# A compressed bias built through DRAM, position weights as the moving operand, and one source for a norm's mean

## The chip, the cores and the metric

The kernel runs on one core of one Trainium2 chip. The metric is the time of one execution on the device, in microseconds (us). Lower is better.

## What is computed

The program is a two-layer decoder step for 512 prompt tokens and 64 new tokens (8 sequences of 8), 576 tokens together, with a stream of 1024 features. Layer 0 is a Mamba-2 mixer with an MLP, layer 1 a sparse attention mixer with an MLP. After each of the four halves stands a post-layer-norm. What the change touches, cut to its core:

```
def layer_norm(x, g, b):
    mu = jnp.mean(xf, axis=-1, keepdims=True)
    var = jnp.mean(jnp.square(xf - mu), axis=-1, keepdims=True)
    return ((xf - mu) * lax.rsqrt(var + LN_EPS)).astype(x.dtype) * g + b

# compression of 32 tokens into one: (token + position vector pe) times w1, per k and v
hid = einsum('bcjgd,jde->bcge', chunks[:, 0:n_cmp] + pe[0:CMP_STRIDE][:, None, :], w1[0]) + (the same for r = 1)
return einsum('bcge,ed->bcgd', silu(hid), w2)

# compressed branch of the attention: a bias by distance, from a table of 32 buckets x 16 heads
s_c = einsum('qgrd,cgd->qgrc', qq, kc) * scale
s_c = s_c + bias_hgr[rel_bucket(pos[:, None] - cmp_end[None, :])]
```

The position vectors' share of the hidden layer, pe times w1, is one vector of 128 for k and one for v: it is summed once and then added as a bias ("position sums").

## The kernel before

**Weights.** All dense products run in `dense_block` (L1247 to L1274). Weights come from DRAM in 512 KB slots. The SP queue loads a slot into one of two `ring` buffers (`stream`, L594 to L599), ScalarE (ACT) rounds it into `split[:, j, 0]` (`split_hi`, L932), GpSimd (POOL) writes the remainder into `split[:, j, 1]` (`split_lo`, L673), and TensorE (PE) then runs 48 matmuls on the slot. So at most four slots are on the way: two in `split`, two in `ring`. SP issues a load only when POOL has split what the ring buffer held, and it issues in program order: any other DMA in its list stands between two slots.

**Bias tables.** Between the first quarter of MLP 0 (its first hidden half) and the second, `bias_tables` (L1503 to L1519) makes on PE first a table `bt` of heads x distances (3 matmuls, L1510) and then the compressed bias `cbt`: 56 matmuls, each with a shifted window of 128 distances of the one-hot table `ef` as the stationary operand and the 32 x 16 bucket table `relb` as the moving one (L1517). VectorE (DVE) copies both out (L2013 to L2019). The next dense block follows on PE at once. SP meanwhile stores `bt` to the DRAM scratch `bscr` (L611), copies it into a skewed table `bskew` (L615), loads strips `Rs` of that (L619) and then 16 small pieces `nr`, one for each head (L624), with slots of weights between these steps. `cbt` is read in the attention, after 1390 us.

**Norms.** `last_projection` (PE), `finish_his` (ACT), `finish_los` (POOL) and `last_residuals` (DVE) build the stream's last eight chunks of 128 features (`xT[:, m]`) with their squares. DVE adds chunks 0 to 6 into `row` while they come. `layer_norm` on PE sums by token (12 short passes for six matmuls, each with 96 tokens as the stationary operand: L1290) `row` and chunk 7 into two columns of `s1`, and the squares into `s2`; spreads the mean over all partitions (L1496, L1497: `row` and chunk 7 accumulate in `flat_x`), and spreads the scale (L1501) when DVE and ACT have computed the variance (L1970 to L1977). DVE then works through eight chunks (L1982, L1985), ACT writes them in two forms (L1106, L1107), and POOL the remainder (L794). Norm k = 1 stands between MLP 0 and the shared K/V projection.

**Position sums.** Their weights `cw1` (2 MB) lie where the bias tables' `ef`, `eb` and `bt` did, and POOL issues the load (L840) behind all its splits of the slots up to norm 1. `position_sums` on PE then stands between the pieces of the first K/V block: 32 matmuls with a 128 x 128 piece of `cw1` as the stationary operand and a single column of `cpe` as the moving one (L1545); PE waits for `cw1` ahead of that block. ACT copies the result as `hpe` (L1110), and PE waits for it before the second block.

An fp32 matmul is two passes of a weight load and a matmul in the trace, so "x112" there is 56 matmuls of the program.

Of the kernel before, what the change touches and what calls it, by code (L numbers as in the profile page):

```python
# [27 lines left out]
ALU = mybir.AluOpType  # L28
ACT = mybir.ActivationFunctionType
AX = mybir.AxisListType  # L30

P = 128
# [53 lines left out]
def build(nc, a):  # L86

    with ExitStack() as ctx:
# [131 lines left out]
        at[0] = KC * T  # L220
        bd = carve(512)
# [54 lines left out]
        CEN, SQS = zip(*((v[:, 0, :], v[:, 1, :]) for v in (spare, spare_x, spare, spare_x)))  # L276
        ptab = sb("ptab", [1, NB * NPG], I32)
# [215 lines left out]
        s1 = dense[0:TQ, 0, 0:2 * TC].rearrange("p (c k) -> p c k", k=2)  # L493
# [96 lines left out]
        def _(sp):  # L590
# [3 lines left out]
            def stream(first, last):  # L594
                with sp.Fori(first // NSLOT, last // NSLOT) as i:
                    for j in range(NSLOT):
# [23 lines left out]
                         ).then_inc(strips_loaded, 16)  # L620
            stream(s_bias + 2 * NSLOT, s_bias + 3 * NSLOT)
            sp.wait_ge(strips_loaded, 16)
# [20 lines left out]
        def _(pool):  # L643
# [194 lines left out]
            pool.wait_ge(cbt_ready, 1)  # L838
# [78 lines left out]
        def _(act):  # L917
# [180 lines left out]
            def layer_norm(k):  # L1098
# [9 lines left out]
                if k == 1:  # L1108
                    act.wait_ge(pe_done, 1)
                    act.activation(hpe, dense[:, 3, 0:2], ACT.Copy).then_inc(hpe_ready, 1)  # L1110
# [133 lines left out]
        def _(pe):  # L1244
# [31 lines left out]
            def projection(b0, s0, blocks, nsl, hi, lo, ready=None, rounded=None, after=None):  # L1276

                for j in range(2):
                    dense_block(b0 + j, s0 + j * nsl, nsl, hi, lo, ready=ready if j == 0 else None,
                                rounded=rounded if j == 0 else None, after=after if j == 0 else None)  # L1280
                    if after and j == 0:
                        pe.wait_ge(hpe_ready, 1)
# [202 lines left out]

            def layer_norm(k):

                b0 = ENDS[k][0]
                pe.wait_ge(ln_sum, 6 * (k + 1))
                by_token(s1, 0, row)  # L1490
                pe.wait_ge(blk_evac, b0 + KC)
                by_token(s1, 1, xT[:, KC - 1, :]).then_inc(ln_tok, 1)
                pe.wait_ge(ln_sq, (k + 1) * KC)
                by_token(s2, 1, sq[:, 1, :]).then_inc(ln_tok, 1)
                for cols in (slice(0, 512), slice(512, T)):
                    pe.matmul(flat_x[:, cols], onesd[:, :], row[:, cols], start=True, stop=False)  # L1496
                    mm = pe.matmul(flat_x[:, cols], onesd[:, :], xT[:, KC - 1, cols], start=False, stop=True)  # L1497
                mm.then_inc(ln_wide, 1)
                pe.wait_ge(ln_stats, 2 * k + 2)
                for cols in (slice(0, 512), slice(512, T)):  # L1500
                    mm = pe.matmul(flat_s[:, cols], ones[0:TQ, :], SQS[k][0:TQ, cols], start=True, stop=True)  # L1501
                mm.then_inc(ln_wide, 1)

            def bias_tables():
# [9 lines left out]
                for i in range(NSIG):  # L1514
                    o_ = i * NH
                    x0 = X0 + CB0 - CS * i
                    mm = pe.matmul(bS[:, o_ // 512, o_ % 512:o_ % 512 + NH], ef[:, x0:x0 + P], relb[:, :],  # L1517
                                   start=True, stop=True)
# [19 lines left out]
            pe.wait_ge(s_cw1, 16)  # L1538

            def position_sums(k):  # L1540


                for j in range(5 * k, min(5 * k + 5, 32)):
                    kv, i = divmod(j, 16)
                    mm = pe.matmul(dense[:, 3, kv:kv + 1], cw1[:, kv, i // 8, i % 8, :],  # L1545
                                   cpe[:, kv, i // 8, i % 8:i % 8 + 1], start=i == 0, stop=i == 15)
                if k == KC - 2:
                    mm.then_inc(pe_done, 1)

            projection(B_KV, S_KV, SL_KV, 1, x_h, x_l, (x_split, 2 * KC), (xh_ready, KC), position_sums)
# [43 lines left out]
            def compressed(s_):  # L1596
                pe.wait_ge(hpe_ready, 1)
# [178 lines left out]
        def _(dve):  # L1776
# [168 lines left out]
            def last_residuals(k):  # L1945
# [13 lines left out]
                for m in range(2, KC):  # L1959
# [3 lines left out]
                    if m < KC - 1:  # L1963
                        dve.wait_ge(blk_evac, b0 + m + 1)
                        dve.wait_ge(ln_sum, 6 * k + m - 1)
# [447 lines left out]
```

## Time and profile before

| | us |
|---|---|
| median of 3 runs | 2146.24 (2142.49 to 2151.03) |
| the profiled execution's own time | 2147.33 |
| its span, first to last instruction | 2145.7 |
| PE busy in it | 1982.5 (92%) |
| PE weight loads | 1817.4 (85%) |
| DVE busy | 866.9 (40%) |
| ACT busy | 652.0 (30%) |
| POOL busy | 973.5 (45%) |
| mean granted TensorE clock | 0.937 of full |

The share of PE tells that the kernel is PE's nearly everywhere; what a change is worth is read from the stretch in which it stands. A granted clock of 1.00 is TensorE's 2.4 GHz, 0.50 is 1.2 GHz.

### The profile page before, as it was taken

Reading aid. Unit: us, or ns where it says so; the run is one execution under the profiler, and the core shown is the slowest. Engines: PE = TensorE matmul, PEld = TensorE weight load, DVE = VectorE, ACT = ScalarE, POOL = GpSimd, SP = SyncE. Lnnn points to the kernel's source line nnn. Section 1 sums busy time; section 2 is a strip of 40 time slices with the busy share of each in tenths; the row PEclk is TensorE's granted clock in tenths of the full one; section 3 lists DMA queues with packets and bytes.
Section 4 is the critical chain, followed back from the end, with each engine's and each line's share of the span. In section 5 each row is a group of like instructions: output and inputs, shape, how many; then the busy total and the mean of one; then the engine's idle time right before and its main releaser. Section 6 shows DMA issues by size and latency. Waiting matters only on the chain.

```text
span 2145.7 us, 36763 instructions
## 1 busy us (share of the span) xinstructions
PE 1982.5 (92%) x14824; PEld 1817.4 (85%) x14824; DVE 866.9 (40%) x1712; ACT 652.0 (30%) x1115; POOL 973.5 (45%) x697
## 2 busy tenths in 40 slices
PE   7989898978979998999999998989978999999997
PEld 5988887857778998999998998955547899999996
DVE  7484766847455210012233112167745621002134
ACT  3443343432133211122223113166634422112222
POOL 2444445446437642356453333344412565345552
PEclk9999999978998988999996998989999899999998
DMA  4211213122131215322221243350060122222221
GB/s 167 71 50 64 104 40 119 50 81 92 50 114 60 81 67 127 100 79 80 87 79 69 79 152 116 87 204 1 21 236 25 56 79 86 81 79 88 79 79 64
DMA packets 52629, 184.61 MB, mean 86 GB/s; under 512 B 7070, under 2 KB 11838, under 8 KB 50976
## 3 DMA queue, kind: packets, MB, share of 16 engines
q1 hardware_dynamic: 40272, 129.66, 18.3%
q0 software_dynamic: 9952, 50.08, 6.5%
q10 hardware_dynamic: 2288, 3.23, 0.4%
q8 instruction: 84, 1.38, 0.3%
q14 instruction: 33, 0.27, 0.0%
HBM read 166.59 MB, written 27.28 MB: 90 GB/s over the span
## 4 chain that ended last, share of the span: by engine, by line
PE 68%; DVE 12%; issue 9%; POOL 5%; ACT 4%; DMA 1%; ACTq 0%; SPq 0%; POOLq 0%; DVEq 0%
PE dense L1269 48%; PE dense L1592 3%; POOL split L673 3%; DVE tile L1908 2%; PE dense L1675 2%; PE bS L1381 2%; DVE tile L1818 2%; PE dense L1632 1%; PE bXM L1662 1%; POOL tile L780 1%; POOL hid L805 1%; PE bXM L1443 1%; PE bXM L1388 1%; PE dense L1710 1%; DVE tile L1811 1%
## 5 line engine op out<-in xcount | busy, mean ns | idle before, releaser
L1269 PE MATMUL dense<-xs,split 128*128 128x288 f32 x6848 | 984.7, 302 | 32.3 <-DVE y_lo L1936 9.2
L1269 PEld LDWEIGHTS dense<-xs,split 128*128 128x128 f32 x6848 | 948.7, 193 | 64.5 <-issue 51.7
L673 POOL TENSOR_TENSOR split<-ring,split 128x1024 fp32r<-128x1024 f32 x212 | 533.6, 2517 | 846.6 <-ACT split L932 825.4
L932 ACT ACTIVATE split<-ring 128x1024 fp32r<-128x1024 f32 x212 | 224.6, 1059 | 830.5 <-PE dense L1269 816.1
L1269 PE MATMUL dense<-hid,split 128*128 128x288 f32 x3072 | 417.1, 298 | 6.0 <-POOL split L673 6.0
L1269 PEld LDWEIGHTS dense<-hid,split 128*128 128x128 f32 x3072 | 415.6, 191 | 6.3 <-POOL split L673 6.3
L1830 DVE SCALAR_TENSOR_TENSOR tile<-tile,dense 128x576 f32<-128x576 f32 (+1 forms) x56 | 42.2, 754 | 422.9 <-PE dense L1269 422.9
L1995 DVE TENSOR_SCALAR sq<-dense 128x576 f32<-128x576 f32 x64 | 48.5, 758 | 310.5 <-PE dense L1269 310.5
L903 POOL TENSOR_SCALAR tile<-tile,tile,tile 128x128 f32<-128x128 f32 (+3 forms) x128 | 78.3, 626 | 80.1 <-DVE tile L2159 80.1
L805 POOL TENSOR_TENSOR hid<-sq,hid 128x576 f32 x64 | 77.2, 1206 | 0.0
L1171 ACT ACTIVATE tile<-tile,tile 128x128 f32<-128x128 f32 (+3 forms) x128 | 70.5, 553 | 18.2 <-DVE tile L2144 18.0
L1818 DVE SCALAR_TENSOR_TENSOR tile<-tile,tile,tile 128x512 f32<-128x512 f32 x72 | 69.5, 966 | 2.6
L1592 PE MATMUL dense<-tile,tile 128*128 128x128 f32 x576 | 66.4, 274 | 0.8 <-issue 0.8
L1592 PEld LDWEIGHTS dense<-tile,tile 128*128 128x128 f32 x576 | 64.9, 188 | 1.9 <-issue 1.2
L1960 DVE SCALAR_TENSOR_TENSOR tile<-tile,tile 128x576 f32<-128x576 f32 x24 | 61.8, 2575 | 0.0
L1118 ACT ACTIVATE hid<-sq 128x576 f32 x64 | 44.0, 687 | 44.3 <-DVE sq L1998 44.3
L1269 PE MATMUL dense<-y_lo,split 128*128 128x288 f32 x256 | 56.1, 301 | 0.0
L1908 DVE SCALAR_TENSOR_TENSOR tile<-tile,tile,tile 128x128 f32<-128x128 f32 (+1 forms) x80 | 53.8, 734 | 0.7
L1632 PE MATMUL dense<-tile,tile 64*128 64x128 f32 (+3 forms) x128 | 47.8, 491 | 6.2 <-DVE tile L2136 4.6
L1675 PE MATMUL dense<-tile,tile 128*64 128x256 f32 x384 | 51.8, 391 | 0.0
L1998 DVE TENSOR_TENSOR sq<-sq 128x576 f32<-128x576 f32 x64 | 48.5, 758 | 2.2
L1632 PE MATMUL bS<-tile,tile 64*128 64x128 f32 (+3 forms) x128 | 48.9, 495 | 0.4 <-DVE tile L2099 0.4
(316 smaller groups left out, 2174.0 us busy)
## 6 DMA issues: line engine op xcount, KB each, us to landing
ring<-in_w SPq DMA_DIRECT2D x212, 512.0 KB, 3.3
tile<-in_state POOLq DMA_DIRECT2D x4, 2048.0 KB, 9.4
o_sssm<-tile POOLq DMA_DIRECT2D x4, 2048.0 KB, 7.5
tile<-in_cmp POOLq DMA_DIRECT2D x32, 256.0 KB, 3.3
tile<-in_win POOLq DMA_DIRECT2D x8, 1024.0 KB, 6.0
tile<-in_sel SPq DMA_DIRECT2D x32, 256.0 KB, 5.1
o_kv<-tile POOLq DMA_DIRECT2D x1, 3456.0 KB, 14.1
bskew<-bscr SPq DMA_DIRECT2D x1, 3072.0 KB, 22.6
```

Source lines behind the costliest of these rows:

```text
L673: pool.tensor_tensor(split[:, j, 1, :], ring[:, j, :], split[:, j, 0, :].bitcast(F32), ALU.subtract).then_inc(w_split, 1)
L805: pool.tensor_tensor(hid[:, 1, m, :], sq[:, j, :], hid[:, 0, m, :].bitcast(F32), ALU.subtract).then_inc(hid_ready, 1)
L903: last = pool.tensor_scalar(pb(u, r)[:, 0:n], pb(u, r)[:, 0:n], wt[:, u % 2, r:r + 1], gate, ALU.mult, ALU.mult)
L932: act.activation(split[:, j, 0, :], ring[:, j, :], ACT.Copy).then_inc(w_hi, 1)
L1171: last = act.activation(pb(u, r)[:, 0:n], pb(u, r)[:, 0:n], ACT.Exp, bias=nmx[:, u % 4, r:r + 1], accum_out=sm[:, u % 4, r:r + 1])
L1269: mm = pe.matmul(dense[:, 2 * par + h_, 0:HT], split[:, j, w, cols], v[:, kk, h_ * HT:(h_ + 1) * HT], start=kk == 0 and t == 0, stop=kk == ...
L1592: mm = pe.matmul(dense[:, 2 * (s_ % 2) + kv, r * P:(r + 1) * P], cw1[:, kv, r, j, :], rows, start=j == 0, stop=j == 7)
L1632: pe.matmul(SB[k][:, 0:(qt + 1) * P], qT[half_of(h_), gp * GR + r, tok(qt)], kvT[half_of(h_), 4 * (br + 1) + gp, 0:(qt + 1) * P], start=Tr ...
L1675: mm = pe.matmul(OBANK[half_of(g), rr * 2 * P:(rr + 1) * 2 * P], v, PT[t % 4][:, h_ * 2 * P:(h_ + 1) * 2 * P], start=br == 0 and kt == 0, ...
L1818: dve.scalar_tensor_tensor(o[:, 0:NP_TOK], r[:, k:k + NP_TOK], cw[:, x, k:k + 1], o[:, 0:NP_TOK], ALU.mult, ALU.add)
L1908: last = dve.scalar_tensor_tensor(yt[:, j * L:(j + 1) * L], xg[:, j, tok(c)], dsk[:, g * 4 + j:g * 4 + j + 1], yt[:, j * L:(j + 1) * L], A ...
L1960: link(dve, "dve", dve.scalar_tensor_tensor(xT[:, m, :], xT[:, m, :], alpha, CEN[k], ALU.mult, ALU.subtract))
```

## The change

Three parts.

1. **Compressed bias.** PE makes 8 matmuls with windows of `ef` that don't overlap, so that a table `btT` of distances x heads results (1024 x 16). DVE copies it out once. SP stores it to `bscr` (rows of 64 bytes) when the skewed table has been made from the old contents, right behind the load of `Rs`, and two slots later waits for that store and issues 56 loads, each of 128 rows of 64 bytes, into `cbt`. DVE waits for them in the attention. POOL's wait ahead of `cw1` now names the matmuls' end.
2. **Position sums.** The column of `cpe` is stationary and 128 columns of `cw1` move. The 32 matmuls stand in norm 1 on PE: 3 behind the last residual, 13 behind the spread mean, 16 behind the spread scale. PE's wait for `cw1` stands ahead of the first 3. The result is one row; ACT copies it to `posr`, and behind the first K/V block two matmuls turn it into two columns, which ACT copies to `hpe`; PE waits for both.
3. **Mean.** DVE adds chunk 7 to `row` as well; PE sums by token and spreads the mean from `row` alone, behind the sums of squares.

```diff
             sp.dma_start(Rs, bass.AP(a["bskew"].tensor, P - 1, [[NH * RW - 1, P], [RW, NH], [1, RB]])
                          ).then_inc(strips_loaded, 16)
+            sp.wait_ge(bt_ready, 2)
+            sp.dma_start(bass.AP(a["bscr"].tensor, 0, [[NH, P], [NH * P, 8], [1, NH]]), btT).then_inc(bt_stored, 16)
             stream(s_bias + 2 * NSLOT, s_bias + 3 * NSLOT)
+            sp.wait_ge(bt_stored, 32)
+            for i in range(NSIG):
+                sp.dma_start(cbt[:, i, :], bass.AP(a["bscr"].tensor, (X0 + CB0 - CS * i) * NH, [[NH, P], [1, NH]])
+                             ).then_inc(cbt_ready, 16)
             sp.wait_ge(strips_loaded, 16)
...
-            pool.wait_ge(cbt_ready, 1)
+            pool.wait_ge(cbt_done, 1)
...
                     act.wait_ge(pe_done, 1)
+                    act.activation(posr[0:1, :], dense[0:1, 2, 0:2 * P], ACT.Copy).then_inc(hpe_ready, 1)
+                    act.wait_ge(pe_done, 2)
                     act.activation(hpe, dense[:, 3, 0:2], ACT.Copy).then_inc(hpe_ready, 1)
...
+                    if b0 == B_KV and j == 0:
+                        position_columns()
+                        pe.wait_ge(hpe_ready, 2)
...
+            def position_sums(first, last):
+                for j in range(first, last):
+                    kv, i = divmod(j, 16)
+                    mm = pe.matmul(dense[0:1, 2, kv * P:(kv + 1) * P], cpe[:, kv, i // 8, i % 8:i % 8 + 1],
+                                   cw1[:, kv, i // 8, i % 8, :], start=i == 0, stop=i == 15)
+                if last == 32:
+                    mm.then_inc(pe_done, 1)
+            def position_columns():
+                pe.wait_ge(hpe_ready, 1)
+                for kv in range(2):
+                    mm = pe.matmul(dense[:, 3, kv:kv + 1], posr[0:1, kv * P:(kv + 1) * P], ones[0:1, 0:1],
+                                   start=True, stop=True)
+                mm.then_inc(pe_done, 1)
+            def fill(k, place):
+                if k == 1:
+                    if place == 0:
+                        pe.wait_ge(s_cw1, 16)
+                    position_sums(*((0, 3), (3, 16), (16, 32))[place])
             def layer_norm(k):
                 b0 = ENDS[k][0]
-                pe.wait_ge(ln_sum, 6 * (k + 1))
-                by_token(s1, 0, row)
                 pe.wait_ge(blk_evac, b0 + KC)
-                by_token(s1, 1, xT[:, KC - 1, :]).then_inc(ln_tok, 1)
+                fill(k, 0)
                 pe.wait_ge(ln_sq, (k + 1) * KC)
                 by_token(s2, 1, sq[:, 1, :]).then_inc(ln_tok, 1)
+                pe.wait_ge(ln_sum, 7 * (k + 1))
+                by_token(s1, 0, row).then_inc(ln_tok, 1)
                 for cols in (slice(0, 512), slice(512, T)):
-                    pe.matmul(flat_x[:, cols], onesd[:, :], row[:, cols], start=True, stop=False)
-                    mm = pe.matmul(flat_x[:, cols], onesd[:, :], xT[:, KC - 1, cols], start=False, stop=True)
+                    mm = pe.matmul(flat_x[:, cols], onesd[:, :], row[:, cols], start=True, stop=True)
                 mm.then_inc(ln_wide, 1)
+                fill(k, 1)
...
                 mm.then_inc(ln_wide, 1)
+                fill(k, 2)
...
-                for i in range(NSIG):
-                    o_ = i * NH
-                    x0 = X0 + CB0 - CS * i
-                    mm = pe.matmul(bS[:, o_ // 512, o_ % 512:o_ % 512 + NH], ef[:, x0:x0 + P], relb[:, :],
+                for i in range(8):
+                    mm = pe.matmul(bS[:, 0, i * NH:(i + 1) * NH], ef[:, i * P:(i + 1) * P], relb[:, :],
                                    start=True, stop=True)
...
-                    if m < KC - 1:
-                        dve.wait_ge(blk_evac, b0 + m + 1)
-                        dve.wait_ge(ln_sum, 6 * k + m - 1)
-                        dve.tensor_tensor(row[:, :], row[:, :], xT[:, m, :], ALU.add).then_inc(ln_sum, 1)
+                    dve.wait_ge(blk_evac, b0 + m + 1)
+                    dve.wait_ge(ln_sum, 7 * k + m - 1)
+                    dve.tensor_tensor(row[:, :], row[:, :], xT[:, m, :], ALU.add).then_inc(ln_sum, 1)
             def layer_norm(k):
                 dve.wait_ge(ln_tok, 3 * k + 2)
-                link(dve, "dve", dve.tensor_reduce(lnt[:, 0, :], s1, AX.X, ALU.add))
-                link(dve, "dve", dve.tensor_tensor(lnt[:, 1, :], lnt[:, 0, :], lnt[:, 0, :], ALU.mult))
+                dve.tensor_reduce(lnt[:, 0, :], s2, AX.X, ALU.add)
                 dve.wait_ge(ln_tok, 3 * k + 3)
-                link(dve, "dve", dve.tensor_reduce(lnt[:, 0, :], s2, AX.X, ALU.add))
+                link(dve, "dve", dve.tensor_copy(lnt[:, 1, :], s1[:, :, 0]))
+                link(dve, "dve", dve.tensor_tensor(lnt[:, 1, :], lnt[:, 1, :], lnt[:, 1, :], ALU.mult))
```

SP's list around the bias tables, before (ring loads are slots of weights, `tile_137` is `Rs`, `tile_117` is `nr`):

```order
L615 DMA bskew<-bscr 2048x1x384
L595 UNCONDITIONAL_BRANCH
L599 DMA ring<-in_w 128x1024 x2
L595 REGISTER_ALU
L595 COMPARE_AND_BRANCH
L619 DMA tile_137<-bskew 128x16x256
L595 UNCONDITIONAL_BRANCH
L599 DMA ring<-in_w 128x1024 x2
L595 REGISTER_ALU
L595 COMPARE_AND_BRANCH
L624 DMA tile_117<-tile_137 8x144 x16
```

The same place of SP's list after the change (`tile_138` is now `Rs`, `tile_118` is `nr`, `tile_115` is `btT`, `tile_132` is `cbt`):

```order
L623 DMA tile_138<-bskew 128x16x256
L626 DMA bscr<-tile_115 128x8x16
L599 UNCONDITIONAL_BRANCH
L603 DMA ring<-in_w 128x1024 x2
L599 REGISTER_ALU
L599 COMPARE_AND_BRANCH
L630 DMA tile_132<-bscr 128x16 x56
L634 DMA tile_118<-tile_138 8x144 x16
L599 UNCONDITIONAL_BRANCH
```

One DMA more stands between two pairs of slots, and 56 more ahead of the 16 that stood there.

PE's list at norm 1, before (`tile_154` holds the summed squares and then the scale, `tile_49` is the stream, `tile_118` is `cpe` and `tile_126` is `cw1`):

```order
L1290 MATMUL dense<-onesd,row 96x1 x6
L1290 MATMUL dense<-onesd,tile_49 96x1 x6
L1290 MATMUL dense<-onesd,sq 96x1 x6
L1496 MATMUL bXM<-row,onesd 128x512
L1497 MATMUL bXM<-tile_49,onesd 128x512
L1496 MATMUL bXM<-row,onesd 128x64
L1497 MATMUL bXM<-tile_49,onesd 128x64
L1501 MATMUL bS<-tile_154,ones 128x512
L1501 MATMUL bS<-tile_154,ones 128x64
L1269 MATMUL dense<-xs,split 128x288 x6
L1545 MATMUL dense<-tile_126,tile_118 128x1 x5
L1269 MATMUL dense<-xs,split 128x288 x6
```

And after the change (`tile_119` is now `cpe`, `tile_127` is `cw1`, `tile_155` the scale):

```order
L1281 MATMUL dense<-hid,split 128x288 x6
L1504 MATMUL dense<-tile_119,tile_127 1x128 x3
L1303 MATMUL dense<-onesd,sq 96x1 x6
L1303 MATMUL dense<-onesd,row 96x1 x6
L1533 MATMUL bXM<-row,onesd 128x512
L1533 MATMUL bXM<-row,onesd 128x64
L1504 MATMUL dense<-tile_119,tile_127 1x128 x13
L1538 MATMUL bS<-tile_155,ones 128x512
L1538 MATMUL bS<-tile_155,ones 128x64
L1504 MATMUL dense<-tile_119,tile_127 1x128 x16
L1281 MATMUL dense<-xs,split 128x288 x48
L1513 MATMUL dense<-ones,row 128x1 x2
```

The position sums moved from inside the first K/V block into the norm, the sums by token of `row` behind those of the squares, and those of the stream's last chunk are gone.

## Rows read from the trace of the kernel before

**Rows 1.** The page: busy us, share of the span and instructions of each engine.

```profile
PE 1982.5 (92%) x14824; PEld 1817.4 (85%) x14824; DVE 866.9 (40%) x1712; ACT 652.0 (30%) x1115; POOL 973.5 (45%) x697
```

**Rows 2.** Timeline 780:818, bias tables: start us, us, engine line op [idle <-releaser].

```profile
787.01 23.10 PE L1517 MATMUL bS<-tile,tile 128*128 128x16 f32 x112 [1.45 <-DVE tile L2015]
...
809.95 8.30 PE L1269 MATMUL dense<-hid,split 128*128 128x288 f32 x42
```

**Rows 3.** Windows: stretch, its length, PE, PEld, DVE, ACT, POOL busy, PEclk, DMA share, GB/s.

```profile
788.00:789.50 1.50, 1.50 (x10) 1.50 (x9) 0.00 (x0) 0.00 (x0) 0.65 (x1) 0.54 0.55 126
...
809.90:815.00 5.10, 5.10 (x23) 5.10 (x23) 1.16 (x2) 0.00 (x0) 0.00 (x0) 0.50 0.00 0
```

**Rows 4.** SP's own timeline, 780:960 (same columns).

```profile
852.21 0.39 SPq L619 DMA_DIRECT2D tile<-bskew  x1
857.04 2.65 SPq L599 DMA_DIRECT2D ring<-in_w  x2
860.93 10.86 SPq L624 DMA_DIRECT2D tile<-tile  x16
872.15 82.05 SPq L599 DMA_DIRECT2D ring<-in_w  x14
```

**Rows 5.** Timeline of all engines, 826:905.

```profile
857.07 48.16 PE L1269 MATMUL dense<-hid,split 128*128 128x288 f32 x338 [6.02 <-POOL split L673]
...
873.11 0.76 DVE L1830 SCALAR_TENSOR_TENSOR tile<-tile,dense 128x576 f32 x1 [21.14 <-PE dense L1269]
...
885.80 1.06 ACT L932 ACTIVATE split<-ring 128x1024 fp32r<-128x1024 f32 x1 [5.34 <-PE dense L1269]
...
886.94 2.38 POOL L673 TENSOR_TENSOR split<-ring,split 128x1024 fp32r<-128x1024 f32 x1 [4.02 <-ACT split L932]
```

**Rows 6.** DMA issues: out<-in, engine, KB each, us to landing.

```profile
ring<-in_w SPq DMA_DIRECT2D x212, 512.0 KB, 3.3
...
tile<-bskew SPq DMA_DIRECT2D x1, 2048.0 KB, 8.7
...
tile<-in_nw ACTq DMA_DIRECT2D x1, 8.0 KB, 6.6
tile<-in_dsk ACTq DMA_DIRECT2D x1, 8.0 KB, 6.3
```

**Rows 7.** Timeline of ACT, 0:40: its DMA issues at the start.

```profile
7.71 0.47 ACTq L923 DMA_DIRECT2D tile<-in_nw  x1
8.21 0.65 ACTq L923 DMA_DIRECT2D tile<-in_dsk  x1
```

**Rows 8.** The chain that ended last, 1120:1180, in order of time.

```profile
1136.11 9.52 DMA tile<-in_cw
```

**Rows 9.** Timeline of norm 1 and the first K/V block, 1119:1200.

```profile
1133.48 2.06 PE L1290 MATMUL dense<-onesd,sq 128*96 128x1 f32 x12
...
1139.70 1.25 PE L1501 MATMUL bS<-tile,ones 96*128 96x512 f32 x4
...
1178.88 1.06 ACT L932 ACTIVATE split<-ring 128x1024 fp32r<-128x1024 f32 x1 [6.57 <-PE dense L1269]
```

**Rows 10.** Windows around norm 1 (columns as in Rows 3).

```profile
1145.60:1171.20 25.60, 25.52 (x113) 25.53 (x114) 6.25 (x9) 8.66 (x13) 8.82 (x8) 0.50 0.00 1
```

**Rows 11.** Timeline of norm 0, 648:700.

```profile
670.65 1.95 PE L1501 MATMUL bS<-tile,ones 96*128 96x512 f32 x4
...
687.66 1.06 ACT L932 ACTIVATE split<-ring 128x1024 fp32r<-128x1024 f32 x1 [1.91 <-PE dense L1269]
```

**Rows 12.** Timeline of the last norm, 2117:2146.

```profile
2121.73 1.23 PE L1290 MATMUL dense<-onesd,tile 128*96 128x1 f32 x12
...
2126.59 1.91 PE L1497 MATMUL bXM<-tile,onesd 128*128 128x512 f32 x2
...
2128.30 0.53 PE L1496 MATMUL bXM<-row,onesd 128*128 128x64 f32 x2
...
2129.05 1.50 PE L1501 MATMUL bS<-tile,ones 96*128 96x512 f32 x4
```

More of the change, by code:

```diff
@@ L220, in build @@
         at[0] = KC * T
+        btT = carve(8, NH)
+        at[0] = KC * T
         bd = carve(512)
@@ L276, in build @@
         CEN, SQS = zip(*((v[:, 0, :], v[:, 1, :]) for v in (spare, spare_x, spare, spare_x)))
+        posr = row[0:1, 0:2 * P]
         ptab = sb("ptab", [1, NB * NPG], I32)
@@ L492, in build @@
         flat_s = bS.rearrange("p a b -> p (a b)")[:, 0:T]
-        s1 = dense[0:TQ, 0, 0:2 * TC].rearrange("p (c k) -> p c k", k=2)
+        s1 = dense[0:TQ, 0, 0:TC].unsqueeze(2)
         s2 = dense[0:TQ, 1, 0:2 * TC].rearrange("p (c k) -> p c k", k=2)
@@ L1274, in dense_block, with projection @@
                     mm.then_inc(w_used, 1)
-            def projection(b0, s0, blocks, nsl, hi, lo, ready=None, rounded=None, after=None):
+            def projection(b0, s0, blocks, nsl, hi, lo, ready=None, rounded=None):
                 for j in range(2):
                     dense_block(b0 + j, s0 + j * nsl, nsl, hi, lo, ready=ready if j == 0 else None,
-                                rounded=rounded if j == 0 else None, after=after if j == 0 else None)
-                    if after and j == 0:
-                        pe.wait_ge(hpe_ready, 1)
+                                rounded=rounded if j == 0 else None)
+                    if b0 == B_KV and j == 0:
+                        position_columns()
+                        pe.wait_ge(hpe_ready, 2)
                 with pe.Fori(1, blocks // 2) as i:
@@ L1536, in _ @@
             layer_norm(1)
[L1538 to L1552, printed above, removed]
+            projection(B_KV, S_KV, SL_KV, 1, x_h, x_l, (x_split, 2 * KC), (xh_ready, KC))
             projection(B_Q, S_Q, SL_Q, 1, x_h, x_l)
@@ L1596, in compressed @@
             def compressed(s_):
-                pe.wait_ge(hpe_ready, 1)
+                pe.wait_ge(hpe_ready, 2)
                 if s_:
@@ L2016, in _ @@
             dve.wait_ge(cbt_done, 1)
-            flat = cbt.rearrange("p s h -> p (s h)")
-            dve.tensor_copy(flat[:, 0:512], bS[:, 0, :])
-            dve.tensor_copy(flat[:, 512:NSIG * NH], bS[:, 1, 0:NSIG * NH - 512]).then_inc(cbt_ready, 1)
+            dve.tensor_copy(btT.rearrange("p s h -> p (s h)"), bS[:, 0, 0:8 * NH]).then_inc(bt_ready, 1)
             residuals(B_M2[0][0], S_M2[0][0], 2, ALPHA)
@@ L2094, in shift_compressed @@
                 dve.wait_ge(pcs_done, qt + 1)
+                dve.wait_ge(cbt_ready, 16 * NSIG)
                 s0 = 24 - 8 * qt
```

## The prediction

> **What bounds the kernel now.** I read the page first: PE is busy 92% of the span [rows 1], so an edit is worth what it takes from PE's line, or what it makes PE wait. Then the timeline of each of three places. At the bias tables PE spends 23.1 us on the 56 shifted matmuls, and the next dense block starts when they end, at 809.95 [rows 2]: all of this is on the path. SP's own timeline behind it shows a queue that already costs something: the load of `Rs` is issued at 852.21, two slots at 857.04, then 16 small DMAs that hold SP for 10.86 us, and the next slot goes out at 872.15 [rows 4]. PE waits 6.02 us for a split slot at 857.07, behind the transfer of the skewed table, but not for the 16 small DMAs [rows 5]: four slots are on the way and cover them. At norm 1 the chain of waits runs through a DMA, not through the norm: `cw1` goes out at 1136.11 and takes 9.52 us, to 1145.63 [rows 8], while the norm's scale was spread by 1140.95 [rows 9]. From there to the end of the first K/V block PE is full for 25.60 us at granted clock 0.50, that is 1.2 GHz [rows 10]; where nothing stands between its pieces, the same block ends 15.1 us behind the spread scale (norm 0: 672.6 to 687.66) [rows 11].
>
> **Part 1a, the matmuls.** 56 become 8, or 112 passes 16. Over all of them a pass takes 23.1 / 112 = 0.206 us [rows 2], early on, partly at full clock, 1.5 / 10 = 0.15 [rows 3]. I take 16 x 0.15 = 2.4, so PE comes free at 789.4: **-20.5 us** (-19.8 by the other pace). Behind the tables the dense block runs at clock 0.50 for 5.1 us [rows 3], which costs some 2.6 us. The clock fell in the first two microseconds of these narrow matmuls, and the 8 lie in them, so I leave that loss as it is; the bound is another -2.6.
>
> **Part 1b, the loads on SP.** I work in the times of the trace of before; the shift is common to all that follows. The store of `btT` goes out behind `Rs` at about 852.7 and can't land before it, 852.21 + 8.7 = 860.9 [rows 4, 6]. Its 1024 rows at the pace of the 2048 rows of `Rs` would add 4.3; the rows are short, I take 863.5 (860.9 to 866). Two slots go out in between as before, at 857.04 and 859.4. Then SP waits for the store and issues 56 loads. What one costs SP no row shows for this queue; the nearest are two loads of the same shape, 128 rows of 64 bytes, that ACT issues in a row at the start: 0.47 and 0.65 us, starts 0.50 apart [rows 7]. `Rs` holds SP 0.39, the 16 pieces 10.86 / 16 = 0.68 each [rows 4]. I take 0.48, nearest to the same shape and a little off it because SP's single issues are shorter: 56 x 0.48 = 26.9 us, to 890.4. The 16 pieces follow, 10.9 us, to 901.3. Only then does the next slot go out: 3.3 us to landing [rows 6], ACT 1.06 and POOL 2.38 [rows 5], with gaps 908.2. PE has worked through its four slots at 885.8 (ACT's rounding starts when the block ends) [rows 5]. So PE waits **22.4 us**. Behind the wait of 6.02 the block of two slots lasts 857.07 to 873.1, 16.0 us, against 12.7 for the one behind it [rows 5]: the clock falls in the wait and costs 3.2. Sum +25.6; with 0.42 for an issue +22.2, with 0.68 +36.8, and the store's landing adds -2.6 to +2.5. The loads themselves land long before `cbt` is read, and DVE's new wait costs nothing.
>
> A rule of the Trainium skill speaks to this (DMA: Bandwidth & Descriptors, Issuing engines are not separate DMA queues): the time that it takes to initiate a DMA on the sequencer is usually small beside the DMA. Here it is the other way: the two small loads land at 7.71 + 6.6 = 14.3 and 8.21 + 6.3 = 14.5, 0.2 us apart, while their issue takes 0.5 [rows 6, 7]. By the rule the 56 would cost what they take to move, 11 us, not 27, and the stall would be 16 us shorter; that is the third rival below.
>
> **Part 1 together:** -20.5 + 25.6 = **+5.1 us**.
>
> **Part 2, norm 1.** What is moved: 64 passes out of the K/V block, into the norm. What moves with them is PE's wait for `cw1`. It stood ahead of the block, it now stands ahead of the sums of squares, and everything in the norm is queued behind it. POOL still issues the load at 1136.1, behind its last split. PE's chain, in the times of before: `cw1` at 1145.6; a 512-column pass at half clock is 1.71 / 2 = 0.85 [rows 12], so one of 128 columns is 0.21 and half of that at full clock; the weight load of one column hides beside it. Three sums, 6 passes: 1.3, to 1146.9. Squares by token 2.06 and `row` by token 2.06 [rows 9], to 1151.0. The mean spread from `row` alone: 1.71 + 0.37 = 2.1 [rows 12], to 1153.1. Then 13 sums, 26 passes: 5.5 at half clock, 2.8 at full; PE has been busy with wide passes for some time by then, I take 4.2, to 1157.3. The scale, which DVE has ready before that, is spread by 1158.5 (1.25 [rows 9]). Before it was 1140.95: **17.6 us later**. The last 16 sums lie beside DVE's first chunks. The block ends 15.1 behind, as at norm 0, at 1173.6; the two column matmuls and ACT's copy, which PE waits for, are some 0.9, so the second block starts at 1174.5 and ends 6.4 later, at 1180.9 (half of the 12.7 of two slots). Before, that end was 1178.88 [rows 9]. So the block's relief of some 14 us is spent on the wait: **+2.0 us**, between +0.6 (full clock) and +4.
>
> **Part 3, the other three norms.** The chunk-7 sums by token took 1.23 and two wide passes 1.71 plus two narrow 0.37 [rows 12]; `row`'s sums by token, formerly hidden beside DVE's last residual, come onto the line with 2.06. In the last norm the scale's spread began 7.3 us behind the last residual, at 2129.05. Now: the square 0.7, squares by token 2.0, `row` 2.0, spread mean 2.1, in sum 6.8; and behind `row`'s sums DVE and ACT need about as long for the scale, 2.1. So -0.3 each, **-1.0 us**. DVE's added row sum lies beside ACT's square and PE's sums of squares. If the scale's chain is met by other work on DVE, +1 each; if PE gets its clock back earlier, -1 each.
>
> **The sum:** +5.1 + 2.0 - 1.0 = +6.1 us on the profiled execution's 2147.33, that is 2153.4. The median of the runs shown is 1.1 lower, so I predict **2152.3**. A change of under 0.5%, 10.7 us, is about what a measurement of this kernel can't tell from none. The forecast's own range, from 0.42 to 0.55 us an issue and the clock, is 2144 to 2159.
>
> **Rivals.** (A) A dear issue: SP takes for each of the 56 what it takes for each of the 16 pieces, 0.68. Then the wait is 56 x 0.20 = 11.2 longer: 2163.5. For it: the same queue, many in a row, short rows. Against: those pieces have SBUF on both sides and only 8 partitions. From 0.57 an issue on the result is beyond 0.5%. Chance 0.28; with a late store it reaches 2168. (B) The four slots cover more than I think and the norm's wait vanishes, because `cw1` lands before the norm: then its sums fill waits, the block ends near 1159 instead of 1173.6, and the time is 2138. Against it is POOL's order, where nothing has moved ahead. Chance 0.05. (C) A cheap issue, at the pace of landing, 0.20: 56 x 0.28 = 15.7 less, 2136.6. For it only that the transfers are that quick; against it every row of an issue here, none under 0.39 [rows 4, 7]. Chance 0.1, a part of it with a gain of over 0.5%. (D) That the change doesn't save the 20 us of PE: nothing speaks for that, since the matmuls are gone from the list; what could eat it is another wait in the same stretch, of a size no row gives. 0.02.
>
> **How the numbers follow.** Forecast 0.55, A 0.28, C 0.1, B 0.05, D 0.02. Within 0.5% lie the forecast, B and most of C; above it A, save its low end, and a tail of the forecast. Faster 0.1, same 0.62, slower 0.28. The range takes in C's edge and A with its late store: 2137 to 2168.
>
> **What would show it.** In the profile after: the dense block behind the tables starts some 20.5 us earlier; SP's timeline shows the 56 in 27 us; PE waits some 22 us for a split, and over 3 at half clock follow; in norm 1 PE waits for `cw1` behind the last residual, for 13 us, and the scale is spread 17 to 18 us later against that residual. The prediction is wrong if an issue costs clearly less or more than 0.48, or if the store of 1024 short rows takes much longer than `Rs`.

## The result, and the profile after

| | before | changed |
|---|---|---|
| median of 19 runs each, us | 2147.22 (2141.58 to 2156.2) | 2154.33 (2146.24 to 2159.42) |
| span of the profiled execution, us | 2145.7 | 2144.6 |
| PE busy in it, us | 1982.5 | 1938.6 |
| mean granted TensorE clock | 0.937 | 0.942 |

The ratio is 1.0031, 95% interval 1.0019 to 1.0043: the changed kernel is slower by 0.3%, or 2147.22 x 0.0031 = 6.7 us (the two medians lie 7.1 apart). The sum had given +6.1. That is less than the 0.5% that the prediction took as the limit of what can be told from none, but 19 runs of each do show the sign.

The page's first rows would tell another story. This is the row of the changed kernel that answers to [rows 1]:

```profile
PE 1938.6 (90%) x14668; PEld 1775.3 (83%) x14668; DVE 864.2 (40%) x1715; ACT 652.8 (30%) x1116; POOL 972.8 (45%) x697
```

PE is busy 44 us less, and nothing is gained. The busy time that went has come back as idle time of the same engine, and two new waits, of 22.6 and 14.6 us, are the most of it (an old wait of 4.7 us for `cw1` went). The view of PE's waits, 775 to 1180, changed kernel (total us, times, longest):

```profile
PE dense L1281 <- POOL split L683: 29.3, 2, 22.6
PE dense L1504 <- DMA tile<-in_cw: 14.6, 1, 14.6
```

The two profiled executions can't be compared as wholes either: the changed one is 1.1 us shorter in its span. It is ahead by 5.5 us before the first changed step of weight. DVE's timeline shows the last residual ahead of norm 0 in the kernel before and then in the changed one:

```profile
662.96 0.75 DVE L1830 SCALAR_TENSOR_TENSOR tile<-tile,dense 128x576 f32<-128x576 f32 x1 [3.53 <-PE dense L1269]
```

```profile
657.43 0.75 DVE L1852 SCALAR_TENSOR_TENSOR tile<-tile,dense 128x576 f32<-128x576 f32 x1 [3.53 <-PE dense L1281]
```

The code up to there (the Mamba half) is the same on PE, so those 5.5 us are nothing that the change did. So I compare stretches between landmarks that both programs have, and take the total from the ratio of many runs. All kernels of this study, by those stretches of their profiled executions (us; "norm 1" is from its last residual to DVE's first copy of the second K/V block; "scale" is from that residual to DVE's first multiplication by the scale):

| kernel | ratio to before, 95% | tables to norm 1 | norm 1 | scale |
|---|---|---|---|---|
| before | 1 | 344.3 | 47.7 | 9.72 |
| changed | 1.0031 [1.0019, 1.0043] | 349.8 | 49.75 | 27.15 |
| p1_alone | 1.0027 [1.0008, 1.0045] | 345.4 | 46.8 | 8.16 |
| p23_alone | 0.9996 [0.9974, 1.0018] | 342.3 | 49.9 | 27.32 |
| late | 0.9910 [0.9881, 0.9939] | 321.6 | 50.2 | 27.63 |
| one_load | 0.9886 [0.9851, 0.9921] | 322.6 | 50.3 | 27.69 |
| cw1_early | 0.9946 [0.9926, 0.9967] | 344.3 | 31.7 | 9.17 |
| best_late | 0.9826 [0.9800, 0.9852] | 321.5 | 36.6 | 14.01 |
| before_cw1_early | 0.9980 [0.9958, 1.0002] | 340.7 | 45.0 | 9.71 |
| p1_late_cw1 | 0.9872 [0.9848, 0.9896] | 323.8 | 45.2 | 9.72 |
| best_one | 0.9842 [0.9812, 0.9872] | 322.4 | 33.4 | 10.83 |
| best_places | 0.9835 [0.9802, 0.9869] | 321.8 | 33.0 | 9.04 |

Each row of stretches is one execution, and not always a middling one. The changed kernel's profiled execution, 2146.24 us, is the quickest of its 19; cw1_early's took 2130.6 (median of its runs 2139.16), and p1_late_cw1's 2131.58 is the slowest of its six (median 2121.95). Behind the bias tables the same 8 matmuls were followed by 6 us at a granted clock of 0.50 in the changed kernel, 0.55 in p1_late_cw1, 0.72 to 0.78 in six other kernels and 1.00 in p1_alone, so between 0 and 3 us of any first stretch is that clock alone.

**The bias tables and SP.** All engines' timeline, 775 to 935, changed kernel, the rows that answer to [rows 2] and [rows 5] (start us, us, engine, line, operation, in brackets idle time and what ended it):

```profile
781.19 2.37 PE L1553 MATMUL bS<-tile,tile 128*128 128x16 f32 x16 [1.45 <-DVE tile L2036]
...
783.39 41.41 PE L1281 MATMUL dense<-hid,split 128*128 128x288 f32 x288
...
831.50 28.48 PE L1281 MATMUL dense<-hid,split 128*128 128x288 f32 x192 [6.70 <-POOL split L683]
...
882.55 41.27 PE L1281 MATMUL dense<-hid,split 128*128 128x288 f32 x288 [22.57 <-POOL split L683]
...
898.38 0.76 DVE L1852 SCALAR_TENSOR_TENSOR tile<-tile,dense 128x576 f32 x1 [37.48 <-PE dense L1281]
```

The 8 matmuls take 2.2 us from their start to the next block's (781.19 to 783.39), where the 56 took 22.94. The wait of 6.02 is still there, as 6.70. Behind it stands the new one, 22.57 us, and it is ended by a split slot. SP's own timeline, 770 to 990, says why (same columns, answers to [rows 4]), and the view of SP's waits, 820 to 900, adds what it waited for ahead of the 56:

```profile
826.68 0.39 SPq L623 DMA_DIRECT2D tile<-bskew  x1
827.12 2.42 SPq L626 DMA_DIRECT2D bscr<-tile  x1
...
837.26 26.71 SPq L630 DMA_DIRECT2D tile<-bscr  x56
864.01 10.85 SPq L634 DMA_DIRECT2D tile<-tile  x16
875.24 110.63 SPq L603 DMA_DIRECT2D ring<-in_w  x19
```

```profile
SPq L630 <- DMA bscr<-tile: 2.9, 1, 2.9
```

From the load of `Rs` to the next slot behind the 16 pieces it was 19.9 us (852.21 to 872.15), and it is 48.6 (826.68 to 875.24). The 28.6 us more are 26.7 for the 56 issues, 26.71 / 56 = 0.477 us each, and the rest is the wait for the store, 2.9 us where SP had waited 1.2 us ahead of the 16 pieces before (857.04 + 2.65 = 859.69, and they go out at 860.93).

**Norm 1.** All engines' timeline 1112 to 1182, changed kernel (answers to [rows 9] and [rows 8]):

```profile
1130.99 0.76 DVE L1852 SCALAR_TENSOR_TENSOR tile<-tile,dense 128x576 f32<-128x576 f32 x1 [9.44 <-PE dense L1281]
...
1135.77 0.56 POOL L850 DMA_DIRECT2D tile<-in_cw  x1
1145.50 1.44 PE L1504 MATMUL dense<-tile,tile 128*1 128x128 f32 x6 [14.62 <-DMA tile<-in_cw]
1146.87 2.08 PE L1303 MATMUL dense<-onesd,sq 128*96 128x1 f32 x12
1148.81 2.06 PE L1303 MATMUL dense<-onesd,row 128*96 128x1 f32 x12
...
1150.73 2.38 PE L1533 MATMUL bXM<-row,onesd 128*128 128x512 f32 x4
...
1153.04 3.77 PE L1504 MATMUL dense<-tile,tile 128*1 128x128 f32 x26
...
1156.74 1.29 PE L1538 MATMUL bS<-tile,ones 96*128 96x512 f32 x4
...
1158.14 0.76 DVE L2006 TENSOR_TENSOR tile<-tile,bS 128x576 f32<-128x576 f32 x1 [4.24 <-PE bS L1538]
...
1173.26 0.76 DVE L2048 TENSOR_SCALAR tile<-dense 128x576 f32 x1 [4.18 <-PE dense L1281]
...
1173.88 8.28 PE L1281 MATMUL dense<-xs,split 128*128 128x288 f32 x60 [0.26 <-ACT tile L1122]
```

PE stands 14.62 us for `cw1` with the whole norm behind that wait. The scale comes 27.15 us behind the last residual instead of 9.72. The first K/V block, without the position sums in it, makes up all but 2.05 us of that: its result is copied 15.12 us behind the scale (1158.14 to 1173.26), where it was 30.33 before.

That 15.1 is the same in all eight kernels with part 2 (15.07 to 15.12 us), with 16 or with 24 sums standing ahead of the block on PE. PE doesn't set it: in the changed kernel it waits seven times, mostly 0.45 us, for the next chunk's remainder from POOL (3.0 us in sum in the view of waits). ACT sets it: it writes each chunk in its two forms, 0.76 us apart and without a gap (ACT's timeline 1160 to 1168), so one chunk comes every 1.52 us. With the sums inside, PE was the bound of the block, busy for 25.52 of 25.60 us [rows 10].

**The last norm.** PE's timeline 2110 to 2146, changed kernel (answers to [rows 12]):

```profile
2122.46 1.15 PE L1303 MATMUL dense<-onesd,sq 128*96 128x1 f32 x12 [1.72 <-ACT sq L960]
2123.47 1.59 PE L1303 MATMUL dense<-onesd,row 128*96 128x1 f32 x12
2124.93 2.37 PE L1533 MATMUL bXM<-row,onesd 128*128 128x512 f32 x4
2127.09 2.35 PE L1538 MATMUL bS<-tile,ones 96*128 96x512 f32 x4
```

The sums by token of chunk 7 and its two wide passes (512 and 64 columns) are gone. From the last residual to the scale it is 8.71 us, before it was 9.73; at norm 0 9.43 against 9.75, at norm 2 10.07 against 9.74. Part 3 was never run alone, and 0.3 us a norm is far below what the runs can tell, so its worth is read from profiles only.

### The profile page after: what moved, and what is told of

Read it like the earlier page. It is cut to its first block and busy times, and to the rows that moved or that the text cites. A ratio compares the mean times of both kernels' runs of the same rounds, so it can differ in the third digit from the quotient of the medians.

```text
span 2144.6 us, 36515 instructions
## 1 busy us (share of the span) xinstructions
PE 1938.6 (90%) x14668; PEld 1775.3 (83%) x14668; DVE 864.2 (40%) x1715; ACT 652.8 (30%) x1116; POOL 972.8 (45%) x697
```

## The experiments

My theory: part 1 gives 21 us on PE and loses a little more than that to SP's 56 issues; part 2's gain is spent on the wait for `cw1`, since POOL issues that load behind its last split. Rivals: the 56 cost by what they move, not by their issue; SP's queue is slowed by something else (the store); the moved sums save nothing of their own.

**Each half alone.** p1_alone is the kernel before with part 1; p23_alone is the changed kernel without it. What parts them, cut short (+ as in p1_alone and the changed kernel):

```diff
+            sp.dma_start(bass.AP(a["bscr"].tensor, 0, [[NH, P], [NH * P, 8], [1, NH]]), btT).then_inc(bt_stored, 16)
...
+            for i in range(NSIG):
+                sp.dma_start(cbt[:, i, :], ...)
...
-                for i in range(NSIG):
-                    mm = pe.matmul(bS[:, o_ // 512, o_ % 512:o_ % 512 + NH], ef[:, x0:x0 + P], relb[:, :], ...)
+                for i in range(8):
+                    mm = pe.matmul(bS[:, 0, i * NH:(i + 1) * NH], ef[:, i * P:(i + 1) * P], relb[:, :], ...)
```

> The kernel before with part 1 alone (8 matmuls, table of distances through DRAM, 56 loads on SP). Theory (SP's issue of the 56 loads starves TensorE of slots): the 56 take 26.7 us on SP, PE waits 22 to 23 us for a split and then runs some 3 us longer at half clock; the matmuls give back 20.7; between the start of the bias tables and the last residual of norm 1 the trace grows by 5.5 us, from 344.3; ratio to before 1.0025. Rival (the loss of the whole change comes from norm 1): no growth here, ratio 0.991 to 1.000.

> The change without part 1 (position sums in norm 1 and the mean from one source alone). Theory: between the bias tables and the last residual of norm 1 the 344.3 us of before; from that residual to the end of the second K/V block 49.6 us against 47.6 before; the three other norms -1.0 in sum; ratio 1.0005. Rival (the wait for cw1 costs more than the block gets back): 1.003 or more.

Measured: p1_alone 1.0027 [1.0008, 1.0045], p23_alone 0.9996 [0.9974, 1.0018]. Both ratios came as expected. As far as the runs can tell, the loss is part 1's: its interval lies above 1, that of parts 2 and 3 around 1. In p1_alone SP holds the 56 for 26.70 us and PE waits 22.0 us at the one place; p23_alone has only the old wait. The view of PE's waits, 785 to 1150, of p1_alone and then of p23_alone:

```profile
PE dense L1277 <- POOL split L681: 28.3, 2, 22.0
```

```profile
PE dense L1495 <- DMA tile<-in_cw: 14.6, 1, 14.6
PE dense L1272 <- POOL split L674: 5.6, 1, 5.6
```

From tables to norm 1 the profile of p1_alone is 1.1 us longer than before, not 5.5 as the changed kernel's. The clock accounts for some 3 of that: behind the 8 matmuls it stayed at 1.00 in p1_alone and fell to 0.50 in the changed kernel, on the same instructions; the two waits for slots are 1.0 us shorter in sum. The windows of that stretch, p1_alone and then changed (stretch, length, busy us of PE, PEld, DVE, ACT, POOL, then the granted clock, DMA share, GB/s):

```profile
788.00:794.00 6.00, 6.00 (x48) 6.00 (x47) 0.10 (x1) 0.00 (x0) 0.00 (x0) 1.00 0.23 86
```

```profile
783.40:789.30 5.90, 5.90 (x25) 5.90 (x26) 0.29 (x1) 0.00 (x0) 0.00 (x0) 0.50 0.20 74
```

**The issue or the transfer?** Two kernels keep all that part 1 computes and moves. late puts the 56 loads behind all weights of the stretch, where `cbt` is still not needed for long; one_load leaves them where they are, but as one DMA of the same 7168 rows of 64 bytes.

```diff
 # late
-            sp.wait_ge(bt_stored, 32)
-            for i in range(NSIG):
-                sp.dma_start(cbt[:, i, :], ...)
             sp.wait_ge(strips_loaded, 16)
...
             stream(s_bias + 3 * NSLOT, S_O + 2 * NSLOT)
+            sp.wait_ge(bt_stored, 32)
+            for i in range(NSIG):
+                sp.dma_start(cbt[:, i, :], ...)
 # one_load
-            for i in range(NSIG):
-                sp.dma_start(cbt[:, i, :], bass.AP(a["bscr"].tensor, (X0 + CB0 - CS * i) * NH, [[NH, P], [1, NH]])
-                             ).then_inc(cbt_ready, 16)
+            sp.dma_start(cbt, bass.AP(a["bscr"].tensor, (X0 + CB0) * NH, [[NH, P], [-CS * NH, NSIG], [1, NH]])
+                         ).then_inc(cbt_ready, 16)
```

> The changed kernel; SP issues the 56 loads behind its last slot ahead of the attention, where it is idle, not between slots. Theory (SP's queue): PE's wait of 22.6 us and the half clock behind it go, the stretch from the bias tables to the last residual of norm 1 falls from 349.8 to 324 us; ratio to before 0.991. Rival (the store of btT or the DMA engines' load of short rows hold the slots): over 335 us.

> The changed kernel with one DMA of 7168 rows in place of the 56 of 128, same bytes, same place. Theory (what holds the slots is SP's time per issue): the wait of PE shrinks by what SP saves against 26.7 us. The store of btT, 1024 rows in one DMA, held SP 2.42 us; by that pace the one load holds it 17 us and PE waits some 13 us; by the 0.39 us of the load of Rs it waits 0 to 3 us. Rival (the DMA engines' time for 7168 short rows holds the slots): PE waits 20 us or more, whatever SP's issue takes, and the slot behind lands late.

Measured: late 0.9910 [0.9881, 0.9939], one_load 0.9886 [0.9851, 0.9921]. The intervals overlap, so the two can't be told apart. The new wait is gone in both, and from tables to norm 1 they take 321.6 and 322.6 us against 349.8. PE's waits up to norm 1, late and then one_load:

```profile
PE dense L1281 <- POOL split L683: 5.9, 1, 5.9
```

```profile
PE dense L1280 <- POOL split L682: 6.4, 1, 6.4
```

And SP's timeline of one_load, with the landing of the one load from the view of DMA issues (KB, us to landing):

```profile
837.93 0.39 SPq L623 DMA_DIRECT2D tile<-bskew  x1
838.37 2.61 SPq L626 DMA_DIRECT2D bscr<-tile  x1
...
847.56 0.38 SPq L629 DMA_DIRECT2D tile<-bscr  x1
847.99 13.60 SPq L633 DMA_DIRECT2D tile<-tile  x16
```

```profile
tile<-bscr SPq DMA_DIRECT2D x1, 448.0 KB, 6.6
```

The same bytes in the same rows hold SP for 0.38 us instead of 26.71 and land in 6.6 us. So it was the number of instructions, neither the transfer nor the store, which stands in both kernels as it was.

The rule of the Trainium skill weighed in the prediction (DMA: Bandwidth & Descriptors, Issuing engines are not separate DMA queues), that initiating is usually small beside the DMA, compares one issue with one transfer, and so read the trace agrees with it: 0.38 us beside 6.6 for the one load, 0.477 beside 1.7 for each of the 56. It doesn't say that the 56 together cost only what they move, as the prediction read it: SP issues them one after the other, and 56 small prices made 26.71 us.

The 16 pieces behind the one load took 13.60 us instead of 10.85, one of them alone 3.56, so a part of the price moved there; four slots on the way cover it.

**The wait for `cw1`.** cw1_early is the changed kernel with POOL's issue of that load ahead of its splits of MLP 0's second quarter and of what follows:

```diff
             mlp_los(0, 0, S_M1[0][1] + 2)
+            pool.wait_ge(cbt_done, 1)
+            pool.wait_ge(bt_stored, 16)
+            pool.dma_start(cw1, a["cw1"]).then_inc(s_cw1, 16)
             mlp_los(0, 1, S_KV + 2)
```

(the three lines behind it go). best_late has both edits, late's and this.

> The changed kernel; POOL issues the load of cw1 ahead of its splits for the second half of MLP 0 instead of behind them. Theory (norm 1 waits for cw1 and for nothing else new): the wait of 14.6 us goes, the second K/V block ends 35.9 us behind the last residual instead of 49.6, 13.7 less than changed; ratio to before 0.9966. Rival (the position sums themselves, some 10 us of passes in the norm, hold the scale's spread): at most 5 us less.

> The changed kernel with both: the 56 loads behind the last slot ahead of the attention, and cw1 loaded ahead of the second half of MLP 0. Theory (two separate waits): the gains add: from the bias tables to the last residual of norm 1 322 us, from there to the end of the second K/V block 31.7; ratio to before 0.982. Rival (the two share a cause, such as the DMA queues): ratio 0.986 or more.

Measured: cw1_early 0.9946 [0.9926, 0.9967], best_late 0.9826 [0.9800, 0.9852]. Against the changed kernel cw1_early gives 0.9946 / 1.0031 = 0.9915, 18 us (give or take 5), and late 0.9879; their product with 1.0031 is 0.9826, best_late's own ratio: the two losses are independent and their removals add (the rival's 0.986 lies outside best_late's interval). In cw1_early's profile the norm stretch is 18.0 us shorter (49.75 to 31.7), where I expected 13.7, the wait. The 4.3 us on top are the clock in this profile, an execution 8.6 us quicker than the median; the runs themselves can't tell 18 from 14. PE's timeline 1120 to 1165, cw1_early, and a window in it:

```profile
1129.14 0.82 PE L1504 MATMUL dense<-tile,tile 128*1 128x128 f32 x6 [0.92 <-DVE tile L1852]
1129.89 1.18 PE L1303 MATMUL dense<-onesd,sq 128*96 128x1 f32 x12
1130.93 1.16 PE L1303 MATMUL dense<-onesd,row 128*96 128x1 f32 x12
1131.95 1.27 PE L1533 MATMUL bXM<-row,onesd 128*128 128x512 f32 x4
1133.16 3.02 PE L1504 MATMUL dense<-tile,tile 128*1 128x128 f32 x26
1136.11 1.30 PE L1538 MATMUL bS<-tile,ones 96*128 96x512 f32 x4
```

```profile
1131.00:1133.00 2.00, 2.00 (x17) 1.52 (x16) 1.00 (x3) 0.00 (x0) 2.00 (x1) 1.00 0.00 0
```

The same five groups take 0.82, 1.18, 1.16, 1.27 and 3.02 us here, and 1.44, 2.08, 2.06, 2.38 and 3.77 behind the wait, 4.3 us more. So behind this wait the norm ran at half clock. But that the wait is what cost it isn't shown: best_late has no wait for `cw1` in this norm, and its profile shows half clock in it all the same (PE's timeline 1100 to 1145, and two windows):

```profile
1107.52 1.44 PE L1504 MATMUL dense<-tile,tile 128*1 128x128 f32 x6 [0.92 <-DVE tile L1852]
...
1115.05 4.33 PE L1504 MATMUL dense<-tile,tile 128*1 128x128 f32 x26
```

```profile
1108.00:1110.00 2.00, 2.00 (x12) 1.39 (x11) 0.26 (x1) 1.13 (x2) 0.79 (x1) 0.50 0.03 8
1118.00:1120.00 2.00, 2.00 (x15) 1.28 (x13) 0.00 (x0) 0.00 (x0) 0.00 (x0) 1.00 0.00 0
```

It costs 36.6 - 31.7 = 4.9 us, and since both profiles show the same instructions in the same order, what decides it is open. Against late, which has the same half clock in its norm, best_late's norm stretch is 13.6 us shorter (50.2 to 36.6), what I expected of the wait alone.

**What are parts 2 and 3 worth when nothing waits?** before_cw1_early is the kernel before with only the early load; p1_late_cw1 is best_late without parts 2 and 3.

```diff
 # before_cw1_early, POOL
             mlp_los(0, 0, S_M1[0][1] + 2)
+            pool.wait_ge(cbt_ready, 1)
+            pool.wait_ge(bt_stored, 16)
+            pool.dma_start(cw1, a["cw1"]).then_inc(s_cw1, 16)
             mlp_los(0, 1, S_KV + 2)
```

> The kernel before with the load of cw1 issued ahead of the second half of MLP 0. Theory: only PE's wait of 4.7 us ahead of the first K/V block goes; ratio 0.998. Rival (the late cw1 set the clock of the block): the block runs at full clock, 15 us less, ratio 0.993.

> The same as the last, without parts 2 and 3: position sums inside the first K/V block with 128 x 128 stationary pieces, two sources for the mean. Theory (moving the position weights pays once cw1 comes in time): from the last residual of norm 1 to the end of the second K/V block 43.5 us, since the block starts 4 us earlier and stays at half clock; 12 to 13 us slower than with parts 2 and 3; ratio to before 0.988. Rival (the block's cost was the late cw1 and the clock it left): under 36 us, no difference to the kernel with parts 2 and 3.

Measured: 0.9980 [0.9958, 1.0002] and 0.9872 [0.9848, 0.9896]. The first is what its theory said. Without part 2 the wait vanishes too, and the norm stretch shrinks only to 45.0 and 45.2 us (43.5 expected for the second). The window of the K/V block in before_cw1_early (in p1_late_cw1 the 20 us from 1130 read the same, 0.50):

```profile
1146.00:1172.00 26.00, 25.34 (x113) 25.00 (x113) 8.49 (x12) 10.97 (x16) 10.53 (x9) 0.50 0.00 1
```

Where the block holds the sums with one moving column, it stayed at clock 0.50, wait or none, though PE was busy throughout; the rival of before_cw1_early, a block at full clock, fell. With 128 moving columns, in the norm, the clock came back within the norm (best_late, 1.00 from 1118 to 1120) or didn't fall (cw1_early). Between p1_late_cw1 and best_late lie 0.0046, or 9.9 us, where I expected 12 to 13 (the two intervals overlap a little; the stretches, 45.2 against 36.6, say 8.6, and 13.5 against cw1_early's 31.7 at full clock). So parts 2 and 3 most likely save some 9 us, and in the changed kernel none of it shows (p23_alone), because the wait stands in the way.

**The two ways together, and the place of the sums.** best_one is one_load with the early load. best_places puts fewer of the 32 sums between the mean and the scale:

```diff
-                    position_sums(*((0, 3), (3, 16), (16, 32))[place])
+                    position_sums(*((0, 3), (3, 8), (8, 32))[place])
```

> The changed kernel with one DMA of 7168 rows for the 56 loads, in their place, and cw1 loaded ahead of the second half of MLP 0. Theory: the same as with the 56 behind the last slot, since neither leaves a wait: stretch from the bias tables to norm 1's last residual 321.5 us, ratio to before 0.9826. Rival (the one load's 7168 rows still disturb the slots beside the early cw1): 0.986 or more.

> The same, with the position sums laid out as 3, 5 and 24 instead of 3, 13 and 16. Theory (the 13 sums ahead of the scale's spread are too many: at half clock they ended 4.4 us behind the scale, at full clock 0.9): from the last residual of norm 1 to its scale 8.3 us at full clock, 9.6 at half, instead of 9.2 and 14.0; 1 to 4 us less, ratio to before 0.9805 to 0.982. Rival (the 24 behind the scale then hold the K/V block): no gain, the second K/V block ends as late as before against the last residual.

Measured: best_one 0.9842 [0.9812, 0.9872], best_places 0.9835 [0.9802, 0.9869]. With `cw1` early the one load and the 56 late ones can't be told apart, as expected; but the rival's 0.986 lies inside best_one's interval too, and against it there is only the profile, in which no new wait is left (6.3 us at the old place). For the places the runs tell nothing: the intervals lie on each other. The profiles show the mechanism (scale 9.04 us behind the last residual, in best_one 10.83), but of these 1.8 us only 0.4 are left at the end of the second K/V block (33.0 against 33.4). The first block keeps all of it; behind it the second takes 8.9 us instead of 7.5, with a mean clock of 0.79 over its first 8 us (1132 to 1140). And the clock differs ahead of the changed place already: PE's timeline 1100 to 1145, best_one and then best_places:

```profile
1108.71 1.27 PE L1532 MATMUL bXM<-row,onesd 128*128 128x512 f32 x4
1109.92 4.67 PE L1503 MATMUL dense<-tile,tile 128*1 128x128 f32 x26
```

```profile
1111.14 2.07 PE L1532 MATMUL bXM<-row,onesd 128*128 128x512 f32 x4
1113.14 2.08 PE L1503 MATMUL dense<-tile,tile 128*1 128x128 f32 x10
```

The same wide mean takes 1.27 in one and 2.07 in the other, so the clock of single executions is of the size of the effect. Inconclusive. The best kernels of the study, best_late, best_places and best_one, can't be told apart: 34 to 37 us below the kernel before by their medians, 1.6 to 1.7%.

## Why the prediction was right

The forecast was 2152.3 and +6.1 us; the runs say 2154.33 and +6.7. The mechanism was right in both places: SP's issues starve PE of slots, and the relief of the K/V block is spent on the wait for `cw1`. That the numbers agree to within 1 us is in part luck, as the clock's share shows. By its steps:

- **The matmuls, -20.5.** From the tables' start to the next block it was 22.94 us and is 2.2: -20.7. The pace of 0.15 us a pass was right (2.4 predicted).
- **The clock behind them, left as it is.** Right for the changed kernel's profile: 0.50 for 5.9 us, as in [rows 3]. But 0.50 is the lowest of the nine profiles that have the 8 matmuls, so this one is the unfavourable end and not the middle. The bound of another -2.6 was real: p1_alone has it.
- **The store.** 10.8 us to landing predicted, 10.1 measured. SP waited 2.9 us for it, and its issue held SP for 2.42, which I hadn't counted: it fell in time that SP had anyway.
- **The 56 issues, 26.9.** 26.71 measured, 0.477 each. The value came from two loads on another engine's queue [rows 7], because their shape was the same; the 16 pieces of the same queue [rows 4] would have misled. late and one_load confirm that the issue is what costs.
- **PE's wait, 22.4, and 3.2 of half clock behind it.** The wait was 22.57. The block of two slots behind it took 15.8 us (882.55 to 898.38), the next one 12.8 (898.38 to 911.18), so the clock cost 3.0.
- **Part 1 together, +5.1.** The stretch between the tables and norm 1 is 5.5 us longer. p1_alone's is 1.1 longer with the clock's 3 us given back, and its runs say +0.0027, 5.8 us. cw1_early has part 1 just as the changed kernel has it, and its stretch is 344.3, no longer than before. So single profiles put part 1 anywhere from 0 to 5.5, and the runs of p1_alone from 2 to 10; +5.1 lies in both, and neither confirms it to the microsecond.
- **Part 2.** Wait 14.6 for 13: `cw1` landed 14.5 us behind the last residual, as I had it, but PE ran dry 0.1 us ahead of that residual (1145.50 - 14.62 = 1130.88) and not over a microsecond behind it. Scale later by 17.4 for 17.6; second block later by 2.05 for 2.0.
- **Part 3, -1.0.** The three norms give -0.32, +0.33 and -1.02 in the changed kernel, in sum -1.0. In late and cw1_early each stands at 9.4 us beside 9.75 before: -0.3, as predicted for a single one, and -1.0 in sum. In the changed kernel norm 2 and the last norm stand off from these 9.4 by the clock, one up and one down, so that its three also give -1.0 is luck.

The sum of the stretches is 5.5 + 2.1 - 1.0 = +6.6, beside +6.7 by the runs; the one is a pair of single executions, and that they agree so closely is luck. That the profiled executions differ by -1.1 in total is the -5.5 of the Mamba half and a -2.1 between the second K/V block and the end, its two norms taken out, both of unchanged code.

**The rivals.** A, the dear issue of 0.68, fell: 0.477. C, the cheap issue, fell for 56 DMAs. What it held, that the transfer is quick, is true, but it needs one instruction to collect it, and then it is worth more than the 16 us that I had priced. The stretch of one_load is 27.2 us shorter: 22.6 for the wait, all of it, 3.0 for the half clock behind it, 0.3 at the older wait, and some 1.3 that are only the clock behind the tables (0.72 there, 0.50 in the changed kernel). B fell for the change, and cw1_early made its condition true. It priced that at 14 us. The profile of cw1_early gives 18.0, with the norm's passes at full clock; best_late beside late gives 13.6, with them at half; the runs give 18, give or take 5. So 14 was the price at half clock, as the prediction had worked it out, and what it left open was the clock, which single executions show either way.

## What to carry to other kernels

Count the DMA instructions of an edit, not its bytes, and multiply by what one holds the issuing queue; then look at which loads stand behind them in that queue and how many are already on the way. Before cutting a repeated product out of the busiest engine, see whether its replacement fits into one DMA with one more dimension. And where a wait moves, ask for what is queued behind it: here the move turned a gain of some 9 us into none, and one load issued earlier on POOL's queue gave some 18 us back by the runs, 14.6 of them the wait. And where a block's own engine is relieved, look at what bounds it next: without the sums the K/V block goes at the pace at which ACT writes the chunks, and took 15.1 us behind the scale in all eight kernels.

## What the runs showed of the hardware that I had not expected

- 56 DMAs of 128 rows of 64 bytes held SP for 26.71 us, one DMA of all 7168 rows for 0.38, and it landed in 6.6 us, less than the 8.8 of `Rs`.
- The store of 1024 rows from 128 partitions held SP for 2.19 to 2.61 us, some six times the load of 2048 rows (0.39), and landed 8.8 to 10.1 us after its issue, behind that load.
- The 16 pieces took 10.85 us of SP behind the 56 small loads, 10.84 with no load of `cbt` ahead of them (late), and 13.60 behind the single one.
- The granted clock on the same instructions varies from one execution to another: behind the tables 1.00 in p1_alone, 0.78 over 6 us in cw1_early, 0.50 in the changed kernel; in norm 1 1.00 in cw1_early and 0.50 in best_late. Half clock at either place costs 3 to 5 us in 2150, so a single profile can't tell an effect of that size from none.
- PE can be busy for 25.34 of 26.00 us and stay at clock 0.50 where matmuls with one moving column stand between its pieces (before_cw1_early).
